# Attention and the output projection of an encoder layer as one interleaved stage on one Trainium2 core, with rows split behind one transpose

## The reference

```python
h = rmsnorm(x); z = h @ w_in                   # 512 Fourier, 512 Q, 128 K, 128 V columns
f = fourier_mix(z[..., :512])                  # 2-D DFT per group of 128, then a linear map
a = banded_attention(q, k, v, sink, rel_bias)  # 8 heads of 64, 2 kv heads, 128-row blocks,
                                               # each block sees 3 key blocks; bias, sink logit
x = x + concat(f, a) @ w_out
t = rmsnorm(x); aff = softmax(t @ w_router)    # 16 experts
gates, idx = top_k(aff.T, 2 * n_tok // 16)     # per group of tokens
ye = (silu(t[idx] @ w_gate) * (t[idx] @ w_up)) @ w_down * gates
y = rmsnorm(x + scatter_add(ye, idx))
```

## Time and profile before

| | |
|---|---|
| median of 3 runs | 3283.11 us (3278.57 to 3286.09) |
| profiled execution, own time | 3282.49 us |
| its span, first to last instruction | 3281.0 us |
| mean granted TensorE clock | 0.946 |
| PE busy | 2929.9 us, 89% of the span |
| DVE, ACT, POOL busy | 1484.1, 1251.0, 308.3 us |
| bytes moved | 464.87 MB |

### The profile page before, as it was taken

The page is one execution under the profiler, slowest core; times in us unless marked ns, Lnnn a source line. Parts: engine busy times, 40 slices in busy tenths (PEclk is TensorE's granted clock), DMA queues, the critical chain, the costliest instruction groups (busy, mean ns, idle before and its releaser), DMA issues. The chain is left out here.

```text
span 3281.0 us, 44215 instructions
## 1 busy us (share of the span) xinstructions
PE 2929.9 (89%) x15423; PEld 2487.1 (76%) x15423; DVE 1484.1 (45%) x2921; ACT 1251.0 (38%) x2109; POOL 308.3 (9%) x256
## 2 busy tenths in 40 slices
PE   7999868687887899926999999999999999999990
PEld 5888767443443788816999999999999999999980
DVE  3221166355564344465445444544445444444334
ACT  3221144365665233312434343334434334333324
POOL 0000000011121000000111111011111111011100
PEclk9999989797999999957999999999999999999995
DMA  5121242223222555533455545455455545455428
GB/s 162 71 95 70 70 128 77 83 81 116 78 80 80 181 192 192 179 118 125 152 174 177 160 147 171 156 185 162 146 174 176 167 140 177 154 181 174 147 75 295
DMA packets 252956, 464.87 MB, mean 142 GB/s; under 512 B 12491, under 2 KB 97644, under 8 KB 243180
## 3 DMA queue, kind: packets, MB, share of 16 engines
q1 hardware_dynamic: 225980, 367.71, 32.2%
q0 software_dynamic: 26928, 96.55, 11.4%
HBM read 358.11 MB, written 106.10 MB: 141 GB/s over the span
## 5 line engine op out<-in xcount | busy, mean ns | idle before, releaser
L1166 DVE TENSOR_TENSOR we_lo<-we_raw,we_hi 128x1024 fp32r<-128x1024 f32 x384 | 467.4, 1225 | 625.9 <-ACT we_hi L1161 625.4
L105 PE MATMUL p_psum<-p_xT_hi,we_hi 128*128 128x384 f32 x2048 | 692.9, 338 | 0.0
L107 PE MATMUL p_psum<-p_xT_hi,we_lo 128*128 128x384 f32 x2048 | 685.3, 335 | 0.0
L106 PE MATMUL p_psum<-p_xT_lo,we_hi 128*128 128x384 f32 x2048 | 685.0, 334 | 0.0
L1161 ACT ACTIVATE we_hi<-we_raw 128x1024 fp32r<-128x1024 f32 x384 | 400.0, 1051 | 6.0 <-DMA we_raw<-w_gate 5.8
L106 PEld LDWEIGHTS p_psum<-p_xT_lo,we_hi 128*128 128x128 f32 x2048 | 384.7, 188 | 0.6
L105 PEld LDWEIGHTS p_psum<-p_xT_hi,we_hi 128*128 128x128 f32 x2048 | 384.4, 188 | 0.6
L107 PEld LDWEIGHTS p_psum<-p_xT_hi,we_lo 128*128 128x128 f32 x2048 | 384.4, 188 | 0.0
L105 PE MATMUL p_psum<-we_hi,p_hid_hi 128*128 128x512 f32 x768 | 300.0, 391 | 0.0
L107 PE MATMUL p_psum<-we_hi,p_hid_lo 128*128 128x512 f32 x768 | 299.0, 389 | 0.0
L106 PE MATMUL p_psum<-we_lo,p_hid_hi 128*128 128x512 f32 x768 | 298.9, 389 | 0.0
(11 more groups left out here) (209 smaller groups left out, 4362.6 us busy)
## 6 DMA issues: line engine op xcount, KB each, us to landing
we_raw<-w_gate SPq DMA_DIRECT2D x32, 2048.0 KB, 7.7
we_raw<-w_up SPq DMA_DIRECT2D x32, 2048.0 KB, 8.0
we_raw<-w_down SPq DMA_DIRECT2D x32, 2048.0 KB, 7.8
h<-p_h_split SPq DMA_DIRECT2D x24, 1024.0 KB, 3.9
zT<-p_z SPq DMA_DIRECT2D x54, 256.0 KB, 2.0
p_x<-x POOLq DMA_DIRECT2D x6, 2048.0 KB, 8.3
p_q_raw<-zT SPq DMA_DIRECT2D x96, 128.0 KB
p_m_raw<-mixT SPq DMA_DIRECT2D x24, 512.0 KB, 4.8
```

The costliest lines, as they stand in the source:

```text
L105: pe.matmul(out, lhi, rhi, start=first, stop=False)
L106: pe.matmul(out, lhi, rlo, start=False, stop=False)
L107: return pe.matmul(out, llo, rhi, start=False, stop=last)
L1166: dve.tensor_tensor(self.lo[:, n % self.HL, ks], self.raw[:, n % self.RAW, ks], self.hi[:, n % self.HL, ks].bitcast(F32), ALU.subtract).th ...
```

## The change

There are three parts.

1. `attention` and `mixer_out` become one stage, `mixer`. It runs over steps s from -2 to 53, written out; step s belongs to unit s, block i = s // 2, and is called even or odd. In a step PE makes the scores of unit s + 1, half of the 48 products of tile i - 1, the transposes of unit s, and on alternate steps the transposes of the normalised row of tile i - 2, the router's product of tile i - 3, and at the end of odd steps the values of both kv heads of block i. These go into the two partition halves of one PSUM bank, and ACT and DVE split that bank straight into `m_hi` and `m_lo`. The Fourier result of the second group is read from SBUF, that of the first from DRAM (`fT`). `w_out` is loaded and split in steps -1 to 2. The bias comes in four transfers. There is no square root on ACT: DVE makes a seed from the bits (three small operations), POOL improves it (`root`, seven linked operations of 128x1), DVE finishes (`norm`). There is one transposed row `h2T`, one PSUM bank E for its halves and the logits.
2. `h2` is stored as plain float32, 1024 words a row. In `experts` 24 transposes per expert replace 48; ACT copies `hi` out of PSUM, and DVE subtracts it from the same bank for `lo`, behind ACT.
3. `routing` finds the logits in SBUF, its 15 turns are written out, and `payload` is made on POOL ahead of and beside the search.

PE's list of a step in `mixer`, and two of its parts:

```diff
+            def step(s, even, i):
+                j, k0 = i - 1, 0 if even else FG
+                if is_unit(s + 1):
+                    scores(s + 1, (0, 1))
+                if is_tile(j):
+                    dense(j, 0, range(k0, k0 + 4))
+                if is_unit(s + 1):
+                    scores(s + 1, (2, 3))
+                if is_unit(s):
+                    turn(s, 0)
+                    turn(s, 1)
+                if even and is_tile(i - 3):
+                    logits(i - 3)
+                if is_tile(j):
+                    dense(j, 1, range(k0, k0 + 2))
+                if is_unit(s) and tiles(i) == 3:
+                    turn(s, 2)
+                if not even and is_tile(i - 2):
+                    turn_h2(i - 2, 1)
+                if is_tile(j):
+                    dense(j, 1, range(k0 + 2, k0 + 4))
+                if even and is_tile(i - 2):
+                    turn_h2(i - 2, 0)
+                if not even and is_unit(s):
+                    values(i)
...
+            def values(b):
+                pe.wait_ge(v_in[b % 2], 16 * (b // 2 + 1))
+                pe.wait_ge(pt_done, turned[2 * b + 2])
+                wait(pe, o_lo_done, b)
+                for i in range(tiles(b)):
+                    for kv in range(NKV):
+                        rows = slice(kv * DH, (kv + 1) * DH)
+                        last = pe.matmul(ps[rows, C], v_sb[:, b % 2, i, rows], pt_sb[:, kv, i], start=i == 0, stop=i == tiles(b) - 1)
+                last.then_inc(pv_mm, 1)
...
+            def turn_h2(j, half):
+                pe.wait_ge(h2_done, j + 1)
+                wait(pe, hT_out, 2 * j + half)
+                wait(pe, lg_out, j)
```

ACT's list of a step in `mixer`:

```diff
+            def step(s, even, i):
+                if even and is_tile(i - 1):
+                    o_high(i - 1)
+                if even and is_tile(i - 2):
+                    squares(i - 2)
+                if is_unit(s):
+                    pt_out(s, 0)
+                    pt_out(s, 1)
+                if is_unit(s + 2):
+                    qk_high(s + 2)
+                if not even and is_tile(i):
+                    f_high(i)
+                if is_unit(s + 1):
+                    exps(s + 1, (0, 1))
+                if is_unit(s) and tiles(i) == 3:
+                    pt_out(s, 2)
+                if is_unit(s + 1):
+                    exps(s + 1, (2, 3))
+                    sink_exps(s + 1)
+                if -1 <= s < WP - 1:
+                    wo_high(s + 1)
+                if even and is_tile(i - 2):
+                    hT(i - 2, 0)
+                if not even and is_tile(i - 2):
+                    hT(i - 2, 1)
```

The norm's root on POOL, and the core of the edits in `routing` and `experts`:

```diff
+            def root(j):
...
+                pool.wait_ge(seeded, 3 * j + 3)
...
+                steps.link(pool.tensor_tensor(t, y, y, ALU.mult))
+                steps.link(pool.tensor_tensor(t, t, v, ALU.mult))
+                steps.link(pool.tensor_scalar(p, t, 0.375, -1.25, ALU.mult, ALU.add))
+                steps.link(pool.tensor_tensor(p, p, t, ALU.mult))
+                steps.link(pool.tensor_scalar(p, p, 1.875, None, ALU.add))
+                steps.link(pool.tensor_tensor(y, y, p, ALU.mult))
+                pool.tensor_tensor(t, y, y, ALU.mult).then_inc(root_done, 1)
...
-            with dve.Fori(0, TURNS) as i:
+            for i in range(TURNS):
...
-                for i in range(2 * KT):
-                    bank, k = i % 8, i // 2
...
+                for k in range(KT):
...
-                    dve.wait_ge(t_mm, e * (2 * KT) + 2 * k + 2)
-                    dve.tensor_copy(xT_lo[:, k], ps[:, (2 * k + 1) % 8, :SLOTS]).then_inc(x_lo_done, 1)
+                    dve.wait_ge(x_hi_done, e * KT + k + 1)
+                    dve.tensor_tensor(xT_lo[:, k], ps[:, k, :SLOTS], xT_hi[:, k].bitcast(F32), ALU.subtract).then_inc(x_lo_done, 1)
```

More of the change, by code:

```diff
@@ L16 @@
+import itertools
 import math
@@ new lines, in exps, with sink_exps @@
+            def exps(u, heads):
+                b, kv = u // NKV, u % NKV
+                act.wait_ge(stat, 2 * u + 1)
+                for h in heads:
+                    row = s_sb[:, kv, h, :tiles(b) * P]
+                    act.activation(row, row, ACT.Exp, bias=nm[:, kv, h:h + 1], accum_out=rs[:, kv, h:h + 1]).then_inc(exp_done, 1)
+            def sink_exps(u):
+                act.wait_ge(stat, 2 * u + 2)
+                act.activation(esum[:, u % NKV], es[:, u % NKV], ACT.Exp).then_inc(exp_done, 1)
@@ L1089, in _, with scores @@
+            dve.wait_ge(const_in, 32)
+            over_steps(step)
         @block.tensor
         def _(pe):
-            def products(t, b, c, ks=range(KT)):
-                if ks[0] == 0:
-                    wait(pe, added, t * 2 - 4 + c + 1)
+            def scores(u, heads):
+                b, kv = u // NKV, u % NKV
+                keys = slice(0, tiles(b) * P)
+                pe.wait_ge(q_lo_done, u + 1)
+                pe.wait_ge(k_lo_done, u + 1)
+                for h in heads:
+                    n, head = u * GH + h, kv * GH + h
+                    wait(pe, added, n - 1)
+                    out = ps[:, A[n % 2], keys]
+                    pe.matmul(out, q_split[:, head], k_hi[:, kv, keys], start=True, stop=False)
+                    pe.matmul(out, q_split[:DH, head], k_lo[:, kv, keys], start=False, stop=True).then_inc(s_mm, 1)
@@ L1123, in _, with logits @@
-            over_steps(pe, step)
+                    last.then_inc(d_mm, 1)
+            def turn_h2(j, half):
+                pe.wait_ge(h2_done, j + 1)
+                wait(pe, hT_out, 2 * j + half)
+                wait(pe, lg_out, j)
+                for k in range(4):
+                    at = 4 * half + k
+                    last = pe.transpose(ps[:, E, k * P:(k + 1) * P], h2_sb[:, at * P:(at + 1) * P], ident[:, :])
+                last.then_inc(ht_mm, 1)
+            def logits(j):
+                pe.wait_ge(hT_out, 2 * j + 2)
+                for k in range(KT):
+                    last = pe.matmul(ps[:, E, :NE], h2T[:, k], wr[:, k], start=k == 0, stop=k == KT - 1)
+                last.then_inc(lg_mm, 1)
@@ L1170, with routing @@
 PAY = 5
-def routing(nc, logits, ranks_d, ident_d, weights, pos_m, payload, onehot_row):
+def routing(nc, ranks_d, ident_d, weights, pos_m, payload, onehot_row):
     ctx, sb, sem, ps = scope(nc, "p5")
@@ L1225, in _ @@
             weights.load_first(sp)
+        @block.gpsimd
+        def _(pool):
+            part = [payload[:, :, :, 2 + i] for i in range(3)]
+            pool.wait_ge(const_in, 32)
+            pool.tensor_copy(payload[:, :, :, 0], ranks[:, P:P + 1].unsqueeze(2).to_broadcast([P, TT, NE]))
+            pool.tensor_copy(payload[:, :, :, 1], ranks[:, P + 1:P + 1 + TT].unsqueeze(2).to_broadcast([P, TT, NE]))
+            pool.wait_ge(aff_done, 1)
+            steps = Steps(pool, parted)
+            steps.link(pool.tensor_copy(part[0], aff[:, :]))
+            steps.link(pool.tensor_tensor(rest[:, :], aff[:, :], part[0], ALU.subtract))
+            steps.link(pool.tensor_copy(part[1], rest[:, :]))
+            steps.link(pool.tensor_tensor(rest[:, :], rest[:, :], part[1], ALU.subtract))
+            steps.link(pool.tensor_copy(part[2], rest[:, :]))
         @block.scalar
@@ L1314, in _ @@
             last.then_inc(aff_t, 1)
-            with pe.Fori(0, TURNS) as i:
+            for i in range(TURNS):
                 pe.wait_ge(cmp_done, (i + 1) * (2 * TRIES))
@@ L1805, in build @@
         left_in = [kept.enter_context(nc.semaphore(f"left_in{i}")) for i in range(weights.RAW)]
[L1806 removed]
+        routing(nc, consts["ranks"], consts["identity"], weights, pos_m, payload, onehot_row)
         experts(nc, weights, consts["identity"], h2, x2, x2_left, left_in, pos_m, payload, onehot_row)
```

781 lines of the change are left out of this document (328 added, 453 removed).

## The result

The median of four runs is 3258.96 us (3256.52 to 3260.93) against 3281.14 us (3278.57 to 3286.09) for the kernel before: a ratio of 0.993 with a 95% interval of 0.9913 to 0.9947, so faster by 0.5% to 0.9%. The forecast was 3219 us in a range from 3155 to 3270: the direction was right and the range held the time, but the gain is 22 us where 63 were forecast. The profiled execution's span is 3259.3 us, against 3281.0 before.

The account below looks back on a forecast made before the run. PE was taken as the bound in experts and mixer_out, with attention leaving it time to fill. Experts -22.0, routing's -5.6, -3.3, -2.0 and -4.5, and the mixer's -26 sum to -63.4 from 3282.5: 3219 us, range 3155 to 3270.

Parts of the forecast that it names:

- Routing: Routing stage: shorter search turns, payload on POOL, logits kept off DRAM and a smaller first gather, -15.4 us together.
- The turns: Routing's search: 14 gaps between turns, at about 0.4 us of DVE idling each, go: -5.6 us.
- The mixer: Merged attention and mixer_out: 778 us against 804, as 50 start, 705 blocks and 23 tail: -26 us.
- PE's work for a block of three tiles, by pitches at full clock: Mixer block: scores, transposes, router, projection and values sum to 27.3 us with no idle time.
- The start: Mixer's start to the end of the first values: 50 us, with w_out split in three steps of about 12 us.
- The first two blocks: Mixer's first blocks: 31.6 us each, less 5 for the first blocks without norm and logits.
- (a): Mixer's values: paired products of the two heads run side by side, -52 us, 3167 us; chance 0.36.
- (c): Mixer stage: granted clock at 0.90, or missed waits, +50 us, 3269 us; chance 0.14.
- The prediction's own sign of being wrong: Mixer: block nearer 29 or 35 us, granted clock below 0.95, or w_out's split holding the start far beyond 50 us.
- Rival (b): POOL's root in the mixer: slow at 0.71 us an operation, 79 us in 22 blocks, 3298 us; chance 0.08.
- The even step's chain: Mixer: the row's transposes wait for norm and logits copy, chain 7.1 us against PE's 5.0, wait 2.1.
- the odd step's wait: Mixer: values wait for the third copy of transposed probabilities, chain 5.8 us against PE's 3.6, wait 2.2.

Follow-up runs that it names:

- the kernel with both moves: Changed kernel with ACT's third copy of transposed probabilities ahead of the next unit's exponentials, and the row's first-half transposes moved into the odd step: 3112.04 us, 0.9461.
- the kernel with both waits filled: Changed kernel plus unused 512-column products in PE's waits, eleven ahead of the values and eight ahead of the row's transposes: 3216.92 us, 0.9793.

## Why the prediction missed

*Experts* (-22.0): right, -22.7. The group takes 2.54 us instead of 2.62, an expert's period fell from 105.2 to 103.7 us.

*Routing* (-15.4): -11.4. The logits' way (2.4 measured, 2.0 forecast) was right; the payload and the first gather together gave 6.0 of 7.8. The turns were mis-sized: the gap of 0.42 was counted whole, but a turn fell from 3.51 to 3.23 us, 0.28, and the first turn took 4.27. In it, POOL makes the payload, and DVE's small operations are longer:

```profile
1433.43 0.82 DVE L1232 TENSOR_TENSOR p_cand<-p_cur,p_bits 128x6 int32<-128x6 int32 x1
...
1437.13 0.53 DVE L1244 TENSOR_TENSOR p_cur<-p_cur,p_best 128x2 f32<-128x2 f32 x1
1437.70 0.17 DVE L1232 TENSOR_TENSOR p_cand<-p_cur,p_bits 128x6 int32<-128x6 int32 x1
```

```profile
1433.18 1.05 POOL L1197 TENSOR_TENSOR p_rest<-p_aff,payload 128x384 f32<-128x384 f32 x1
1434.29 1.26 POOL L1198 CAST payload<-p_rest 128x384 bf16<-128x384 f32 x1
```

*The mixer* (-26): +9.5, and here two steps failed. One is "PE's work for a block of three tiles, by pitches at full clock": the lower clock behind the waits stood at nothing in the sum, and costs some 39 us. The other is the start: the split of w_out was to be over with the first values, but two of its four pieces come behind them, in two blocks that take 18 us more than forecast. The pieces of the sum, each against its measure:

- The start, 50 us to the end of the first values: 50.5 (611.3 to 661.8).
- The 21 blocks from 734.2: forecast 21 x 31.6 less 17 for the three shorter ones, 646; measured 660.9. Three errors lie in this sum, and they cancel in part. *PE's work* at full clock was 563 (21 x 27.3, less the shorter blocks' share of 10.5); the kernel with both moves, which hardly waits, takes 527.5 for it (726.7 to 1254.2): -35. *The waits* were 84 (21 x 4.3, less 6.6) and are 94 (51.1 ahead of the values, 42.9 ahead of the row's transposes): +10. *The clock* was nothing; 660.8 less 527.5 and 94 leaves 39: +39. By the granted clock PE is at half for 102 us of the stretch.
- Per block of three tiles, PE's work is 25.5 us where 27.3 were forecast. The pairs give 2.5 of that (the values take 2.73 where 5.2 were booked). Against it, the 48 projection products take 11.9 where 10.9 were booked from an unbroken row of them: the first one behind a product of another form has a pitch of 0.32 to 0.34 us instead of 0.23 (from the kernel with both moves):

```profile
1031.99 0.44 PE L1005 MATMUL p_psum<-p_k_lo,p_q_split 64*128 64x384 f32 x1
1032.36 0.50 PE L106 MATMUL p_psum<-p_wo_hi,p_m_hi 128*128 128x512 f32 x1
1032.70 0.40 PE L107 MATMUL p_psum<-p_wo_lo,p_m_hi 128*128 128x512 f32 x1
1032.93 0.39 PE L108 MATMUL p_psum<-p_wo_hi,p_m_lo 128*128 128x512 f32 x1
```

- The first two blocks, forecast 2 x 31.6 less 5, 58: measured 76. Four steps split w_out, not three, and they are not 12 us but 17 apart (the low part starts at 631.7, 648.5, 666.3 and 684.0), two of them behind the first values. The first period after it is 41.6 us. PE waits four times in these two blocks, 17 us in all where two blocks of the forecast have 8.6, for DVE's maxima, for the low part of the last piece, for the copies and for the row, and the granted clock averages 0.81:

```profile
670.96 0.66 PE L1005 MATMUL p_psum<-p_k_hi,p_q_split 128*128 128x384 f32 x1 [4.33 <-DVE p_mx L912]
...
686.44 0.76 PE L106 MATMUL p_psum<-p_wo_hi,p_m_hi 128*128 128x512 f32 x1 [6.11 <-DVE p_wo_lo L896]
...
699.78 4.49 PE L1023 MATMUL p_psum<-p_pt,p_v 128*64 128x512 f32 x12 [3.19 <-issue]
...
718.01 1.11 PE L1049 MATMUL p_psum<-p_ident,p_wo_raw 128*128 128x128 f32 x4 [3.77 <-DVE p_wo_raw L960]
```

  Moving the low part behind the division took 3.9 us from the first of these periods; what sets the rest of the 17 us per step was not tested.
- The tail, 23 us behind the last values: 28 (1397.0 to 1424.9), in part at the lower clock.

So rivals (a) and (c) both came true, where the prediction had each by itself: the gain of the one was eaten by the other. That a block came out near the forecast 31.6 us is luck. The prediction's own sign of being wrong was there: a granted clock of the stage below 0.95, and the steady part has 0.92. That the waits cause the half clock is shown by the runs: take both away (0.9461), or fill both (0.9793), and the granted clock is 1.0 in the steady part; fill one, and it stays at 0.92. A block with both waits and hardly any half clock lasts 30.3 us, 25.5 + 4.9; the average of 32.6 is the clock's. So the waits cost more than the 4.3 us a block that was booked, since a part of them is paid a second time in clock. Of the difference between the change and both moves (0.993 to 0.9461, some 154 us; 147 by the medians), the waits themselves are 54 + 47 us (the sums of idle time ahead of the values and of the row's transposes, without 0.8 at the first values and 5.6 in the tail that stay); the kernel with both waits filled, which waits for the same results, gained 45 us by the ratios, and that is the clock. Rival (b) was wrong: the root's operations take 0.19 to 0.21 us. That attention and its output projection can fill each other was right, and worth more than forecast once nothing waits: 1284.1 - 614.9 = 669 us for the stage with both moves, against 804 before.

The even step's chain was right in its parts (7.3 us from the router's first record to the row's transposes, 7.1 forecast). The trace names the copy of 16 logits (`pos_m`) as what ended the wait, but that is the last by 0.1 us only: the norm itself, which the transposes need too, ends at 1069.48 and the copy at 1069.57. It is the chain through the norm that PE waits for, and moving the transposes, not the copy, took the wait away.

One size of the odd step's wait is open. DVE's statistics, 0.2 in the forecast, took 0.89 to 0.94 us in all 23 odd steps in which POOL split the Fourier part, and 0.17 in even ones:

```profile
1066.63 0.17 DVE L919 TENSOR_SCALAR p_nm<-p_mx 128x4 f32<-128x4 f32 x1
...
1080.45 0.90 DVE L919 TENSOR_SCALAR p_nm<-p_mx 128x4 f32<-128x4 f32 x1
```

```profile
1080.07 1.26 POOL L784 TENSOR_TENSOR p_m_lo<-f_sb,p_m_hi 128x512 fp32r<-128x512 f32 x1
```

It ends with POOL's operation (1081.35 and 1081.33). The Trainium skill, GPSIMD Engine Reference, section 1 (Specifications), says that POOL's SBUF interfaces are shared with VectorE, with contention where the DVE instruction is in a 2-port perf mode or has two SBUF inputs. This one has a single input, and the trace does not show its mode, so the cause is not shown. The 0.7 us could account for the wait of 2.75 instead of 2.2; moving the split elsewhere was not tried.

## What to carry to other kernels

When independent work is interleaved on PE, price its records at both clock levels, and look for every place where PE waits for another engine: here 94 us of waits cost some 40 us more in clock. A copy or a transpose that stands one place late in an engine's list can cost far more than its own time; two such moves were worth here nearly seven times what the whole change was. Filling one wait with work did not help here while another was left.

## What the runs showed of the hardware that was not expected

Products in the two column halves of the array do run beside each other: six records alone take 2.72 us, twelve in pairs 2.73. PE also ran records beside each other that are not neighbours in its list: with eight records, all of one head and then all of the other, the group took 1.87 us in either order, so the fifth began beside the first; with twelve it took 3.63 us, the first two records alone and pairs from the third on. Both fit a reach of four places, which is read from these times and not tested further. So "nothing is reordered", as it stands ahead of the prediction, does not hold for the starts of these records. The Trainium skill, TensorEngine Tiling (Array Packing), section Key Properties, has the first of these, and the runs agree with it.

In the steady part of the changed kernel the lower clock came in stretches of about 3.5 us (some of 7) that began from 0.8 us before to 2.4 us behind the end of a wait of PE of 1.9 to 2.8 us, not behind each one; with one of the two waits filled it came behind the other, for as long in all.
